# S5 branch: input matrices turned by VectorE in 32x32 squares, angles computed one pair ahead by GpSimd

## What is computed

```python
dt = exp(log_dt); mag = exp(a_re * dt)
lr, li = mag * cos(a_im * dt), mag * sin(a_im * dt)     # per group: 64 complex states
bbr, bbi = ...                                          # input matrices, from lr, li, a, b
xr = einsum('bsgc,gnc->bsgn', u, bbr); xi = einsum('bsgc,gnc->bsgn', u, bbi)
h_t = lam * h_(t-1) + x_t                               # complex and diagonal, 2048 steps
y = Re(C h) + D u
```

## Time and profile before

| | before |
|---|---|
| median of 3 runs | 2207.67 us |
| lowest and highest | 2206.61, 2209.12 us |
| profiled execution, own time | 2208.02 us |
| its span in the trace | 2206.4 us |
| TensorE busy | 2185.9 us (99%) |
| VectorE busy | 1372.9 us (62%) |
| ScalarE busy | 938.3 us (43%) |
| GpSimd busy | 148.2 us (7%) |
| granted TensorE clock, mean | 0.998 of full speed |

### The profile page before, as it was taken

One profiled execution on the slowest core, in us unless ns is written; L12 is line 12 of the kernel. 1 busy time (PEld: TensorE's weight loads), 2 busy tenths in 40 slices (PEclk: granted clock), 3 DMA queues, 4 the chain that ended last, 5 costly groups with the idle time before them and its releaser, 6 DMA issues.

```text
span 2206.4 us, 29493 instructions
## 1 busy us (share of the span) xinstructions
PE 2185.9 (99%) x10488; PEld 1780.9 (81%) x10488; DVE 1372.9 (62%) x2795; ACT 938.3 (43%) x1373; POOL 148.2 (7%) x268
## 2 busy tenths in 40 slices
PE   9999999999999999999999999999999999999997
PEld 6788888888888888887777777888888888888886
DVE  7700058778778778756666656256567566665756
ACT  6511145545545545533333333244444354354344
POOL 0000000000000000011111111111002001200100
PEclk9999999999999999999999999999999999999999
DMA  6422111111111111022222222366337536734732
GB/s 214 107 71 71 48 63 58 34 43 57 34 42 57 34 42 48 20 96 80 84 83 81 91 81 84 93 216 191 122 119 244 171 94 190 227 111 129 224 115 76
DMA packets 140108, 223.25 MB, mean 101 GB/s; under 512 B 38832, under 2 KB 82608, under 8 KB 140016
## 3 DMA queue, kind: packets, MB, share of 16 engines
q1 hardware_dynamic: 119936, 160.39, 24.1%
q0 software_dynamic: 20080, 61.64, 7.9%
HBM read 166.25 MB, written 54.53 MB: 100 GB/s over the span
## 4 chain that ended last, share of the span: by engine, by line
PE 90%; DVE 5%; ACT 2%; issue 2%; DMA 1%; SPq 0%; DVEq 0%; ACTq 0%
PE c_bank L107 28%; PE c_bank L108 27%; PE c_bank L109 27%; PE c_bank L457 1%; DVE hg_ken L722 1%; PE c_bank L470 1%; PE c_bank L468 1%; PE c_bank L447 1%; PE c_bank L1153 1%; PE c_bank L1141 1%; PE c_bank L1149 1%; DVE n_sumsq L846 1%; DMA x_xs<-x_in 0%; PE c_bank L1130 0%; ACT c_w_both L522 0%
## 5 line engine op out<-in xcount | busy, mean ns | idle before, releaser
L107 PE MATMUL c_bank<-u_hi,c_w_both 128*128 128x512 f32 x1216 | 487.4, 401 | 3.0 <-DVE u_lo L829 1.9
L109 PE MATMUL c_bank<-u_hi,c_w_both 128*128 128x512 f32 x1216 | 473.6, 390 | 0.0
L108 PE MATMUL c_bank<-u_lo,c_w_both 128*128 128x512 f32 x1200 | 468.3, 390 | 0.0
L107 PEld LDWEIGHTS c_bank<-u_hi,c_w_both 128*128 128x128 f32 x1216 | 228.2, 188 | 73.3 <-issue 20.6
L109 PEld LDWEIGHTS c_bank<-u_hi,c_w_both 128*128 128x128 f32 x1216 | 228.3, 188 | 48.9
L108 PEld LDWEIGHTS c_bank<-u_lo,c_w_both 128*128 128x128 f32 x1200 | 225.5, 188 | 42.8 <-issue 0.2
L1746 ACT ACTIVATE c_w_both<-c_raw 128x1024 fp32r<-128x1024 f32 x90 | 95.5, 1061 | 180.4 <-PE c_bank L109 169.7
L722 DVE STREAM_TRANSPOSE hg_ken<-hg_ke 32x128 f32<-32x128 f32 x512 | 154.8, 302 | 6.5
L1200 ACT ACTIVATE s_stage<-c_bank 128x512 f32<-128x512 f32 x80 | 47.7, 596 | 207.4 <-PE c_bank L109 182.8
L109 PE MATMUL c_bank<-t_oa_hi,c_w_both 128*128 128x512 f32 (+1 forms) x344 | 132.1, 384 | 0.0
L107 PE MATMUL c_bank<-t_oa_hi,c_w_both 128*128 128x512 f32 (+1 forms) x344 | 132.1, 384 | 0.0
(11 more groups left out here) (332 smaller groups left out, 4555.2 us busy)
## 6 DMA issues: line engine op xcount, KB each, us to landing
c_raw<-w_in_in SPq DMA_DIRECT2D x44, 512.0 KB, 4.1
gates_scratch<-s_stage POOLq DMA_DIRECT2D x64, 256.0 KB, 2.7
t_ein<-gates_scratch SPq DMA_DIRECT2D x64, 256.0 KB, 4.4
c_raw<-w_o_hg_in SPq DMA_DIRECT2D x32, 512.0 KB, 3.9
c_raw<-w_out_in SPq DMA_DIRECT2D x32, 512.0 KB, 3.7
c_raw<-w_ple_gate_in SPq DMA_DIRECT2D x32, 512.0 KB, 3.5
iv_rows_scratch<-n_iv_stage SPq DMA_DIRECT2D x32, 256.0 KB, 2.3
hg_ivn<-iv_rows_scratch SPq DMA_DIRECT2D x32, 256.0 KB, 2.8
```

Of the source, the lines that this page charges most:

```text
L107: pe.matmul(out, w_hi, u_hi, start=first, stop=False)
L108: pe.matmul(out, w_hi, u_lo, start=False, stop=False)
L109: return pe.matmul(out, w_lo, u_hi, start=False, stop=last)
```

## The change

- `angles` leaves VectorE. GpSimd computes them (`angles` in gpsimd) with 13 tensor_tensor operations on 128x256, each waiting for the one before it by semaphore, into one half of a doubled `trig`. In the slot of pair p it computes the angles of pair p + 1, ahead of store_y and of the four stores, after hp_done of pair p - 1. In the slot of pair 0 it first computes those of pair 0, and then those of pair 1.
- The two TensorE transposes and ScalarE's copy of `px` go. VectorE turns `X` straight into `w_in_t` with 16 transposes of [32, 2, 32] (`turn_inputs`), in the place of `angles`.
- TensorE's wait for xz_done comes after two K steps of tile 1 instead of three, and the third K step lies between the wait and the multiplication of Z by bb.
- ScalarE waits once, at slot 4, for the staged tiles of the z slots.

```diff
-        trig = m.sb("trig", [P, 2, NCK])
+        trig, ta, tb = m.sb("trig", [P, 2, 2, NCK]), m.sb("ta", [P, NCK]), m.sb("tb", [P, NCK])
+        rounder = m.sb("rounder", [P, 2])
...
+            def angles(p, r):
+                n = [0]
+
+                def link(ins):
+                    n[0] += 1
+                    ins.then_inc(turned_angle, 1)
+                    pool.wait_ge(turned_angle, p * 12 + (ANGLE0 + n[0]))
...
+                if not is_at(p, 0):
+                    pool.wait_ge(ang_done, p)
+                each = lambda x: x.to_broadcast([P, NCK])
+                link(pool.tensor_tensor(ta[:], nn[:], each(f_hi[:, pc]), ALU.mult))
+                link(pool.tensor_tensor(tb[:], ta[:], each(rounder[:, 0:1]), ALU.add))
...
+                pool.tensor_tensor(cos, ta[:], tb[:], ALU.subtract).then_inc(ang_done, 1)
...
             def body(b, p, r, z):
                 if is_at(b, 1):
                     constants()
+                if is_at(p, 0):
+                    pool.wait_ge(par_dve, 11)
+                    angles(0, 0)
+                if p is not None and (not isinstance(p, int) or p + 1 < PAIRS):
+                    if not is_at(p, 0):
+                        pool.wait_ge(hp_done, p)
+                    angles(p + 1, 1 - r)
                 if p is not None and not is_at(p, 0):
                     store_y(p - 1, 1 - r)
...
                 project(b, r, 0)
-                project(b, r, 1, range(0, 3))
+                project(b, r, 1, range(0, 2))
                 if not first:
                     pe.wait_ge(gelu_done, p)
                 pe.wait_ge(xz_done, p + 1)
-                for q in range(2):
-                    pe.transpose(px[:, q * P:(q + 1) * P], X[:, q].rearrange("p j c -> p (j c)"), c["ident"][:])
+                project(b, r, 1, range(2, 3))
...
                     act.wait_ge(ang_done, p + 1)
-                    act.activation(trig[:], trig[:], ACT.Sin, scale=TWO_PI).then_inc(trig_done, 1)
-                    act.wait_ge(mats_done, p + 1)
-                    act.activation(w_in_t[:].rearrange("p k n -> p (k n)"), px[:, 0:2 * P], ACT.Copy).then_inc(turned_done, 1)
+                    act.activation(trig[:, r], trig[:, r], ACT.Sin, scale=TWO_PI).then_inc(trig_done, 1)
                 for t in range(NT):
                     act.wait_ge(proj_done, b * NT + t + 1)
+                    if is_at(b, Z_BLOCKS) and t == 0:
+                        act.wait_ge(staged, Z_BLOCKS * NT)
...
-                def angles():
...
+                def turn_inputs():
+
+                    rows = X[:].rearrange("p k j c -> p k (j c)")
+                    for i in range(P // SQ):
+                        for j in range(P // SQ):
+                            ins = dve.transpose(w_in_t[j * SQ:(j + 1) * SQ, :, i * SQ:(i + 1) * SQ],
+                                                rows[i * SQ:(i + 1) * SQ, :, j * SQ:(j + 1) * SQ])
+                    ins.then_inc(turned_done, 1)
```

More of the change, by code:

```diff
@@ L950, in vector, with part_s5 @@
             return last_step
-        return Part(sync, gpsimd, tensor, scalar, vector, drained=[(sigf, STEPS), (sg_done, STEPS), (iv_staged, 2 * TOKENS), (qe_done, STEPS)],
+        return Part(sync, gpsimd, tensor, scalar, vector, pool_chain=(mk, 5), drained=[(sigf, STEPS), (sg_done, STEPS), (iv_staged, 2 * TOKENS), (qe_done, STEPS)],
                     over=[(last_out, 16), (o_out, 16 * STEPS - 16)])
-def part_s5(nc, c, a, w, banks, u_hi, u_lo, drained, head_over):
+def part_s5(nc, c, a, w, banks, u_hi, u_lo, drained, head_over, pool_chain):
     NB, Z_BLOCKS, AHEAD = 20, S5KT, 2
@@ L998, in part_s5 @@
         ysb = m.sb("ysb", [P, 2, 2, NCK])
-        ps, py, px, pin = banks[0:NT], banks[4:6], banks[6], banks[7]
+        ps, py, pin = banks[0:NT], banks[4:6], banks[7]
         raw_in, w_hi_done, w_lo_done, proj_done = w.raw_in, w.hi_done, w.lo_done, m.sem("proj")
@@ L1020, in part_s5 @@
         is_at = lambda x, n: isinstance(x, int) and x == n
+        turned_angle, ANGLE0 = pool_chain
         def sync(sp):
@@ L1070, in constants @@
                           allow_small_or_imprecise_dtypes=True).then_inc(consts_done, 1)
+                pool.memset(rounder[:, 0:1], MAGIC)
+                pool.memset(rounder[:, 1:2], 0.25)
                 pool.memset(w_intra[:], 0.0).then_inc(zeroed, 1)
@@ L1073, in constants @@
                 pool.wait_ge(zeroed, 2)
+            def angles(p, r):
[4 more added lines that the diff above has]
+                    pool.wait_ge(turned_angle, p * 12 + (ANGLE0 + n[0]))
+                pc = ds(p, 1)
+                sin, cos = trig[:, r, 0], trig[:, r, 1]
+                if not is_at(p, 0):
[3 more added lines that the diff above has]
+                link(pool.tensor_tensor(tb[:], ta[:], each(rounder[:, 0:1]), ALU.add))
+                link(pool.tensor_tensor(tb[:], tb[:], each(rounder[:, 0:1]), ALU.subtract))
+                link(pool.tensor_tensor(ta[:], ta[:], tb[:], ALU.subtract))
+                link(pool.tensor_tensor(tb[:], nn[:], each(f_lo[:, pc]), ALU.mult))
+                link(pool.tensor_tensor(ta[:], ta[:], tb[:], ALU.add))
+                link(pool.tensor_tensor(tb[:], ta[:], each(rounder[:, 0:1]), ALU.add))
+                link(pool.tensor_tensor(tb[:], tb[:], each(rounder[:, 0:1]), ALU.subtract))
+                link(pool.tensor_tensor(sin, ta[:], tb[:], ALU.subtract))
+                link(pool.tensor_tensor(ta[:], sin, each(rounder[:, 1:2]), ALU.add))
+                link(pool.tensor_tensor(tb[:], ta[:], each(rounder[:, 0:1]), ALU.add))
+                link(pool.tensor_tensor(tb[:], tb[:], each(rounder[:, 0:1]), ALU.subtract))
+                pool.tensor_tensor(cos, ta[:], tb[:], ALU.subtract).then_inc(ang_done, 1)
             def store_y(p, r):
@@ L1262, in parameters @@
                 par(dve.tensor_tensor(si[:], si[:], den[:], ALU.mult))
-            LINKS = 38
+            LINKS = 30
             def pair(p, r, first):
@@ L1278, in pair @@
                 chan = lambda x, nj: x.to_broadcast([P, nj, GC])
-                sin, cos = trig[:, 0], trig[:, 1]
+                sin, cos = trig[:, r, 0], trig[:, r, 1]
                 def matrices():
@@ L1348, in states @@
                     dve.sem_inc(hp_done, 1)
-                return matrices, angles, taps, states
+                return matrices, turn_inputs, taps, states
             def gated(b, t):
@@ L1356, in body @@
                 if p is not None:
-                    matrices, angles, taps, states = pair(p, r, is_at(p, 0))
+                    matrices, turn_inputs, taps, states = pair(p, r, is_at(p, 0))
                     matrices()
-                    angles()
+                    turn_inputs()
                 if z:
@@ L2025, in build @@
             head = part_head(nc, c, a, w, banks, xs, u_hi, u_lo)
-            s5 = part_s5(nc, c, a, w, banks, u_hi, u_lo, head.handed_on["drained"], head.handed_on["over"])
+            s5 = part_s5(nc, c, a, w, banks, u_hi, u_lo, head.handed_on["drained"], head.handed_on["over"],
+                         head.handed_on["pool_chain"])
         tail = part_tail(nc, c, a, w, banks, s5.handed_on)
```

9 lines of the change are left out of this document (removed).

## The result

The changed kernel takes 2214.06 us (median of 9 runs, 2211.86 to 2216.49) against 2207.12 us for the kernel before (9 runs beside them): ratio 1.0030, 95% interval 1.0021 to 1.0038, 0.3% slower. The forecast was 2243.0 us. The profiled execution took 2214.55 us with a span of 2212.9 us, 6.5 us more than the one before.

A forecast was written before the change was run, and what follows sets the result against it. TensorE was taken to bound the kernel. 2208.0 (profiled) - 4.65 transposes + 8.6 and 3.4 in pair 0 + 28.0 in the loop = 2243.4, as a median 2243.0 us; range 2209 to 2264.

The forecast's parts named there:

- Bounds of the kernel: TensorE bounds the kernel, busy 2185.9 of 2206.4 us; work it drops in the loop is saved whole, waits lost whole.
- Transposes: Dropping TensorE's transpose pair saves 0.31 us a slot, counted for 15 slots: 4.65 us.
- Earlier wait, and turning on VectorE: Asking for xz_done one K step earlier has 1.0 us of loop slack; VectorE's 16 transposes, at most 4.8 us, are hidden.
- Angles on GpSimd: GpSimd's 13 linked operations take 0.90 us a link, 11.7 us for one pair; bounds 4.7 to 13.
- First pair: Pair 0's angles come late, so TensorE waits for states: +8.6 us; disturbed states and split add +3.4 us.
- 14 x 2.0 = 28 us: In 14 slots GpSimd's angles hold up VectorE's operations, 0.55 us each, costing TensorE 2.0 us a slot.
- early placement: GpSimd's angles start with VectorE's matrices: seven operations, 3.9 us, less 1.0 of slack, make 2.9 us of wait a slot.
- late placement: GpSimd, running late, meets VectorE's states: eight operations, 4.4 us, less 2.6 us of slack, make 1.8 us a slot.
- The rule of the Trainium skill: A VectorE instruction with two SBUF inputs and a GpSimd one reading SBUF exclude each other for a whole instruction.
- Rival 1: The engines do not disturb each other: profiled 2212.0 us, median 2211.6, +0.18%; chance 23%.
- Rival 2: Cheap angles, links below 0.60 us, and no disturbance: ends at or below the time before, 2205.1 or 2204.7 us; chance 7%.
- Rival 3: GpSimd's queue becomes the bound, last eight or so slots 29.6 us: 2254 us, or 2264 with 1.0 us links; chance 12%.

The follow-up runs named there:

- experiment 2: Changed kernel, but GpSimd computes pair 0's angles one slot earlier, between the second and third store of slot 1: 2252.4 us, ratio 1.0207.
- experiment 5: Changed kernel with GpSimd's angles kept, but TensorE's transposes, ScalarE's copy and the xz_done wait after three K steps as before: 2215.94 us, ratio 1.0039.
- experiment 9: Changed kernel with pair 0 wholly as before the change, and GpSimd starting each slot's angles only after that slot's matrices (xz_done): 2206.03 us, ratio 0.9993.
- experiment 1: Changed kernel, but VectorE computes pair 0's angles itself, ahead of its 16 transposes; GpSimd computes those of pairs 1 to 15: 2206.95 us, ratio 0.9998.
- experiment 6: Kernel of experiment 2 plus one wait: GpSimd begins a slot's angles only after that slot's matrices on VectorE are done (xz_done): 2210.88 us, ratio 1.0017.
- experiment 4: Changed kernel, but VectorE computes all angles, ahead of the 16 transposes, and GpSimd none: 2211.33 us, ratio 1.0017.
- experiment 8: Kernel of experiment 1, but in pair 0 TensorE waits for xz_done after three K steps instead of two: 2207.59 us, ratio 1.0000.

## Why the prediction was wrong

Against the forecast sum, the profiled executions show: transposes -3.4 us instead of -4.65; the first pair +7.1 instead of +8.6 and +3.4; the loop 0 instead of +28; and two terms that the sum did not have, +2.3 us of half clock and 0.45 us from before the slot.

**Bounds of the kernel: right.** TensorE's wait in pair 0 was lost whole, and with the transposes gone every slot became shorter.

**Transposes: mis-sized.** 0.23 us a slot, not 0.31; 3.4 us in all. The pair starts 0.31 us before the multiplication of Z by bb. Without it that multiplication starts 0.32 us after the last projection matmul (991.17 and 991.49), where a projection matmul or a transpose would start 0.23 us after it; so 0.09 us of the 0.31 stay. TensorE's idle time ahead of the multiplication rose from 2.7 to 5.6 us over 16 slots. That the transposes had covered its weight loads would explain it, but is not shown.

**Earlier wait, and turning on VectorE: right in the loop.** No wait for xz_done or w_in_t in any slot but the first, and there for xz_done alone; a transpose is 0.24 us where 0.303 was the bound. In pair 0 the wait for xz_done was 1.5 us, and the clock fell behind it; TensorE's stream was slow until 995.5, hidden here by the longer wait later on.

**Angles on GpSimd: mis-sized.** 9.4 us a pair, not 11.7. The operation was well bounded (0.61 and 0.73 us, forecast 0.66); the gap to the next was 0.08 us, not the 0.24 of L331. The estimate from the Trainium skill's figure (GPSIMD Engine Reference, section Elementwise — side-by-side cycle accounting) was 0.56 us before the start's own cost: the trace agrees roughly.

**First pair: right in mechanism, too high in size.** The chain was the forecast one: last store, angles, ScalarE's sine at 1000.53 instead of 993.77, sigmoid, rounding, split, states, L1186. 8.6 + 3.4 = 12.0 us were forecast and 7.1 measured: 6.0 by the late angles, as the links were shorter, and 1.1 us of held-up states instead of 3.4. The 2.3 us of half clock were named beforehand as a thing "which nothing above counts".

**"14 x 2.0 = 28 us": the step that failed.** It measured 0. The forecast took the disturbance for 0.55 us a met operation, and experiment 2 shows +0.25 to +0.5 (0.29 to 0.31 became 0.55 to 0.78), so the price was a little high. The prediction said that GpSimd would start with the matrices or, once late, in the states, that it would change between the two, and that both cost about 2 us after their slack. Two things were wrong in that. First the placement: the changed kernel was late in every slot, so the 2.9 us of the early placement were never due. Second the size of the late placement: eight held-up operations, 4.4 us, less 2.6 us of slack, were to cost 1.8 us a slot. Measured were 0 to 2.2 us of delay, from at most seven held-up steps of 0.1 to 0.6 us each (the scan counted as two); most of GpSimd's 13 operations fell on the transposes, on operations that read a PSUM bank, or on idle VectorE. The slack covered it. Experiments 5 and 9 show how close that was: at 2.4 to 2.6 us of delay TensorE loses 0.1 to 0.3 us a slot. In the early phase the forecast would have been near: experiment 2, at 2252.4 us, lies within its range, with slots of 28 and 30 us. That the changed kernel stayed in the late phase was not foreseen, and the slot of pair 3 shows that little was missing.

**The rule of the Trainium skill** (SBUF — State Buffer, section Who interferes with whom): two SBUF inputs on VectorE against a reading GpSimd exclude each other. The runs agree. Disturbed: two-tile operations, in experiment 2 from 307 to 658 ns in the median. Undisturbed: the transposes (236 ns in the changed kernel and in experiment 2) and L1366 with a bank and a tile (425). It also says that the order of issue decides who blocks. That fits the slot of pair 3, where VectorE's L1252 began at 1080.31 and kept its 1.23 us, and GpSimd's L1098, begun at 1080.42, took 1.58 us instead of 0.61. The one-tile copy and tensor_scalar that experiment 2 shows held are not covered by the sentence on two inputs. The rule has no word on how many operations meet or what this costs a kernel, so the prediction's "By that rule the sum is as here" took it for a confirmation of a size that it does not give.

**Rivals.** Rival 1's number (2211.6) was nearest, by another cause and so by luck: the engines do disturb each other, where it costs nothing. Rival 2 asked for links under 0.60 us; they took 0.72 us start to start. Rival 3's queue was real in kind: from one start of the angles to the next GpSimd took 24.6 to 28.1 us, against a slot of 25.97. That can keep its lateness from melting; it drifted to 11.7 us and bounded nothing.

## To carry to other kernels

When work moves to an engine that can hold up another, list for each operation of the moved work which of the other's operations it will overlap. In this kernel the operations with two SBUF tiles as inputs paid, and some with one tile, a copy and a tensor_scalar; transposes and operations that read a PSUM bank did not. Slack decides the rest. A queue nearly as long as the loop's period may settle early or late in it: in experiments 1 and 2 a few us in the first turn went with a phase that lasted for the whole loop. So keep it off the operations that must not meet it with a semaphore (experiment 6: one wait, 41.5 us) rather than leave its place to chance. And look at the first turn by itself: work done "one ahead" is not ahead there, and here that turn ate nearly three times what 15 later ones gave (9.4 us against 3.4).

## What was not expected of the hardware

- TensorE's clock fell to half behind idle times as short as 1.55 us (changed kernel, 0.63 us a matmul from 992.0 on), 1.69 us (experiment 1) and 1.89 us (experiment 2), and it did not fall behind 1.84 us (experiment 4), 1.91 us (experiment 2) and 1.94 us (experiment 8). So the length of the idle time alone does not decide it; the runs do not show what does. Unused matmuls in the gap kept it at full.
- Linked GpSimd operations follow each other within 0.08 us.
- The same program took 2206 to 2208 us in nine executions and 2248 to 2250 in two (experiment 8), on one core.
